# One decoder layer on one core: the SSM output moved behind the mask product, the merge's first loads split over two queues, the expert records loaded before the expert stage

## The reference, cut to what matters

```
h = rms_norm(x)
proj = h @ w_in                        # all branch inputs and 3 x 1024 gate logits
y_gla, y_hgrn = chunked gated linear attention (8 heads, per-channel decays)
y_ssm = rms_norm((ssd_scan(xs, dt, B, C) + d * xs) * silu(z))   # Mamba-2, 16 heads
merged = sum over 3 branches of sigmoid(gates[b]) * (y_b @ w_br_b)
x = x + merged @ w_out
h = rms_norm(x)
x = x + top-2-of-32 experts (group top-1, then 2 of 8), SwiGLU, weighted
out = rms_norm(x)
```

## Time and profile before

| | us |
|---|---|
| median of 3 runs | 2226.93 (2224.96 to 2229.48) |
| the profiled execution | 2230.12, its span 2228.3 |
| PE busy in the span | 1998.3 (90%) |
| DVE / ACT / POOL busy | 1325.1 / 940.3 / 367.8 |
| mean granted clock of PE, 1.0 = 2.4 GHz | 0.954 |

### The profile page before, as it was taken

How to read it: one execution, slowest core, us unless ns; L and a number is a source line. 1 busy time by engine, 2 the same in 40 slices (tenths; PEclk the granted TensorE clock), 3 DMA queues, 4 the chain that set the end, 5 groups by cost and what they waited for, 6 DMA issues and landing times. The chain is left out here.

```text
span 2228.3 us, 25317 instructions
## 1 busy us (share of the span) xinstructions
PE 1998.3 (90%) x10102; PEld 1664.4 (75%) x10103; DVE 1325.1 (59%) x1426; ACT 940.3 (42%) x1012; POOL 367.8 (17%) x209
## 2 busy tenths in 40 slices
PE   4999999999989999989997999985599999999970
PEld 3778888888978777777775788775488888888860
DVE  4740000576115777767873665565599999999945
ACT  5120101112114433444442334242578888888842
POOL 3213323243410000000000100011122222222200
PEclk9999999999989999999998999997699999999995
DMA  4133222123235543654543754451799999999947
GB/s 154 59 144 102 98 91 95 59 93 132 76 101 144 144 136 115 158 140 144 148 133 126 259 210 185 150 220 48 255 370 381 387 387 387 390 385 385 388 181 264
DMA packets 218988, 435.85 MB, mean 196 GB/s; under 512 B 30770, under 2 KB 153666, under 8 KB 191234
## 3 DMA queue, kind: packets, MB, share of 16 engines
q1 hardware_dynamic: 185698, 354.63, 45.9%
q10 hardware_dynamic: 21152, 54.53, 6.7%
q0 software_dynamic: 12032, 25.22, 3.0%
HBM read 369.67 MB, written 81.43 MB: 202 GB/s over the span
## 5 line engine op out<-in xcount | busy, mean ns | idle before, releaser
L583 DVE TENSOR_SCALAR tap<-u,taps 128x1024 f32<-128x1024 f32 x16 | 20.1, 1298 | 294.0 <-ACT u L541 294.0
L613 PE MATMUL ps<-h_hi,w_hi 128*128 128x512 f32 x576 | 178.4, 391 | 4.8 <-PEq L58 4.8
L613 PE MATMUL ps<-h_lo,w_hi 128*128 128x512 f32 x576 | 178.4, 391 | 0.0
L613 PE MATMUL ps<-h_hi,w_lo 128*128 128x512 f32 x576 | 178.3, 391 | 0.0
L2296 DVE TENSOR_TENSOR gu_lo<-gate_raw,gu_hi 128x2048 fp32r<-128x2048 f32 x64 | 146.7, 2293 | 48.1 <-ACT gu_hi L2243 48.1
L1247 PE MATMUL psum<-h_hi,l_hi 128*128 128x512 f32 x384 | 160.5, 418 | 7.3 <-PEq L58 7.3
L1247 PE MATMUL psum<-h_lo,l_hi 128*128 128x512 f32 x384 | 161.0, 419 | 0.0
L1247 PE MATMUL psum<-h_hi,l_lo 128*128 128x512 f32 x384 | 160.6, 418 | 0.0
L2296 DVE TENSOR_TENSOR gu_lo<-up_raw,gu_hi 128x2048 fp32r<-128x2048 f32 x64 | 146.3, 2288 | 13.4 <-ACT gu_hi L2243 13.4
L2301 DVE TENSOR_TENSOR dn_lo<-dn_raw,dn_hi 128x2048 fp32r<-128x2048 f32 x62 | 142.0, 2292 | 16.0 <-ACT dn_hi L2253 13.0
L551 ACT ACTIVATE out<-ps 128x2048 f32<-128x2048 f32 x14 | 26.4, 1883 | 271.1 <-PE ps L613 202.1
(11 more groups left out here) (352 smaller groups left out, 5024.3 us busy)
## 6 DMA issues: line engine op xcount, KB each, us to landing
gate_raw<-moe SPq DMA_DIRECT2D x66, 1024.0 KB, 8.8
up_raw<-moe SPq DMA_DIRECT2D x64, 1024.0 KB, 8.4
dn_raw<-moe SPq DMA_DIRECT2D x62, 1024.0 KB, 7.8
w_raw<-w_in SPq DMA_DIRECT2D x26, 1024.0 KB, 6.7
dn_raw<-w_br SPq DMA_DIRECT2D x16, 1024.0 KB, 7.5
l_raw<-w_gates ACTq DMA_DIRECT2D x24, 512.0 KB, 4.9
s_gates<-l_out ACTq DMA_DIRECT2D x48, 256.0 KB, 4.0
gate<-s_gates SPq DMA_DIRECT2D x16, 768.0 KB, 5.4
```

The source lines that it names most:

```text
L583: ins = nc.vector.tensor_scalar(tap[:, a, :], u[b][:, a, 0:T], taps[b][:, a, 0:1], None, ALU.mult)
L613: ins = nc.tensor.matmul(ps[b][:, a * T + half * 512:a * T + half * 512 + 512], w[:, k, a * P:(a + 1) * P], h[:, k, half * 512:half * 512 ...
```

## The change

It has four parts.

1. `mixers`: DVE's `ssm_out(c - 1)` moves from ahead of the `k_in` product to behind the mask product `wmat * cbm`; DVE waits for its own `yb_ready` before it overwrites `yt`. On PE one of the two slots of fill that stood behind the `k_in` transposes moves ahead of them.
2. Start of `merge_and_route`: step 0's weights are loaded and split in two halves; the eight first-half y pieces get eight buffers of their own (pieces 4 to 7 in `xh`) and eight semaphores, the even ones issued by ACT and the odd ones by SP, with no wait; POOL issues the second half's pieces only. The table is filled from `h2T` instead of `xh[0]`.
3. Routing on ACT: the first `exps` moves behind the last sigmoid, and a table set that holds both Ln and Exp is preloaded before it.
4. `recs` becomes a buffer that outlives the block: SP loads it at the end of `merge_and_route`, after the last scatter, as two transfers (experts 0 and 1, then the other 30). In the expert block ACT no longer waits for it, POOL waits for the first part only, and DVE zeroes `xe` instead of POOL.

```diff
@@ mixers, DVE
                 dec(i0 + 8)
-                if c:
-                    ssm_out(c - 1)
                 dve.wait_ge(e_ready, NE * c + NE)
...
                 tt(w4, w4, cbm[:]...).then_inc(w_ready, 1)
+                if c:
+                    ssm_out(c - 1)
                 dec(i0 + 9)
                 dec(i0 + 10)
...
                 dve.wait_ge(inter_ready, c + 1)
+                if c:
+                    dve.wait_ge(yb_ready, c)
@@ mixers, PE
                 level(c, 6)
-                fill(SLOT)
+                fill(2 * SLOT)
...            # six transposes of k_in
-                fill(2 * SLOT)
+                fill(SLOT)
@@ merge_and_route, SP
-            weights(0)
+            sp.dma_start(first(w0_raw), first(io["w_br"][0])).then_inc(w0_loaded, 16)
+            y_piece(sp, 1)
+            y_piece(sp, 3)
+            sp.dma_start(second(w0_raw), second(io["w_br"][0])).then_inc(w_loaded[0], 16)
+            y_piece(sp, 5)
+            y_piece(sp, 7)
             weights(1)
...
             sp.wait_ge(work_stored, 16)
+            sp.wait_ge(scattered, 16 * 2 * NCH)
+            places = dr["table"].rearrange("(e s) w -> s e w", s=T)[0:SLAB]
+            sp.dma_start(recs[:, 0:2, :], places[:, 0:2, :]).then_inc(recs_first, 16)
+            sp.dma_start(recs[:, 2:N_EXPERTS, :], places[:, 2:N_EXPERTS, :]).then_inc(recs_in, 16)
@@ merge_and_route, ACT
+            for p in range(0, PIECES, 2):
+                y_piece(act, p)
             nc.scalar.preload_act_table(ACT.Sigmoid)
...
                 upper_w(step_of(n) + 2)
-                if n == 2 * DM - 2:
-                    exps(0)
+            nc.scalar.preload_act_table_set(EXP_LN_SET)
+            exps(0)
@@ experts_first_slabs
-            sp.dma_start(recs[:], dr["table"]...).then_inc(recs_in, 16)      # SP
-            for b in range(2):                                               # POOL
-                nc.gpsimd.memset(xe[b][:], 0.0).then_inc(zeroed, 1)
-            pool.wait_ge(recs_in, 16)
+            pool.wait_ge(recs_first, 16)
-            act.wait_ge(recs_in, 16)                                         # ACT, ahead of gate_up(0, 0)
+            for b in range(2):                                               # DVE
+                nc.vector.memset(xe[b][:], 0.0).then_inc(zeroed, 1)
```

More of the change, by code:

```diff
@@ L1542, in merge_and_route, with y_piece @@
         block = ctx.enter_context(nc.Block())
+        def y_piece(eng, p):
+            half, q = divmod(p, PIECES)
+            if half:
+                eng.wait_ge(y_ready, p - 7 if p < PIECES + 4 else p - 3)
+            eng.dma_start(y_part(p), dr["y"][q * PK * P:(q + 1) * PK * P, half * HT:(half + 1) * HT]
+                          .rearrange("(k p) t -> p k t", p=P)).then_inc(y_second[p % 4] if half else y_first[p], 16)
+        W0 = 8 * P
+        first = lambda t: t[:, 0:W0]
+        second = lambda t: t[:, W0:2048]
+        w0_raw = w_raw[0][:].rearrange("p k n -> p (k n)")
         @block.sync
@@ L1632, in _ @@
         def _(pool):
[L1633 to L1644, removed]
+            nc.gpsimd.memset(h2T[:].rearrange("p k t -> p (k t)").bitcast(U32), EMPTY).then_inc(empty_ready, 1)
             nc.gpsimd.iota(it32[:], pattern=[[1, N_EXPERTS]], base=0, channel_multiplier=0, allow_small_or_imprecise_dtypes=True).then_inc(const_ready, 1)
@@ L1701, in upper_w, with upper_w0 @@
                 nc.scalar.copy(out, w_raw[s % 2][:].rearrange("p k n -> p (k n)")).then_inc(w_hi_ready, 1)
+            def upper_w0(part, loaded, ready):
+                act.wait_ge(loaded, 16)
+                nc.scalar.copy(part(w_hi[0][:]), part(w0_raw)).then_inc(ready, 1)
             def upper_y(p):
-                act.wait_ge(y_loaded[p % 4], 16 * (p // 4 + 1))
+                if p < PIECES:
+                    act.wait_ge(y_first[p], 16)
+                else:
+                    act.wait_ge(y_second[p % 4], 16 * ((p - PIECES) // 4 + 1))
                 if p >= PIECES:
@@ L1741, in exps @@
                 nc.scalar.activation(e2[:, 0:n], e2[:, 0:n], ACT.Exp).then_inc(pick_exp, 1)
-            upper_w(0)
-            for p in range(PIECES):
+            upper_w0(first, w0_loaded, w0_hi_ready)
+            for p in range(4):
+                upper_y(p)
+            upper_w0(second, w_loaded[0], w_hi_ready)
+            for p in range(4, PIECES):
                 upper_y(p)
@@ L1891, in places, with rest_w0 @@
                     nc.vector.tensor_copy(rec[:, pick, cs, 2].bitcast(F32), w[:, 0:n]).then_inc(rec_ready, 1)
-            rest_w(0)
-            for p in range(PIECES):
+            def rest_w0(part, hi_ready, ready):
+                dve.wait_ge(hi_ready, 1)
+                tt(part(w_lo[0][:]), part(w0_raw), part(w_hi[0][:]).bitcast(F32), ALU.subtract).then_inc(ready, 1)
+            rest_w0(first, w0_hi_ready, w0_ready)
+            for p in range(4):
+                rest_y(p)
+            rest_w0(second, w_hi_ready, w_ready)
+            for p in range(4, PIECES):
                 rest_y(p)
@@ L2324, in body @@
                                         hT_hi[:].rearrange("p k t -> p (k t)").bitcast(F32), ALU.subtract).then_inc(hT_split, 1)
+            for b in range(2):
+                nc.vector.memset(xe[b][:], 0.0).then_inc(zeroed, 1)
             for p in range(GU):
```

51 lines of the change are left out of this document (32 added, 19 removed).

## The result

| | before | after |
|---|---|---|
| median, us | 2226.86 (4 runs, 2224.96 to 2229.48) | 2202.31 (4 runs, 2196.90 to 2209.94) |
| the profiled execution, its span | 2230.12, 2228.3 | 2209.94, 2208.2 |
| mean granted clock of PE | 0.954 | 0.958 |

The ratio is 0.9887 with a 95% interval of 0.9866 to 0.9907, so 20.7 to 29.8 us less, 25.2 by the ratio itself. The profiled execution after the change is the slowest of its four; the trace therefore shows a gain of 20.2 us where the medians differ by 24.6. What sets it apart from the fastest is mostly PE's clock. Call (1 - granted clock) x span the clock deficit of an execution: it is 92.7, 92.5, 85.7 and 79.0 us in the four executions of 2209.94, 2204.91, 2199.72 and 2196.90 us. The ratios further down leave out two of merge_only's twelve executions (2650 and 6410 us), which were disturbed, and no others.

The account below looks back on a forecast made before the run. PE, busy for 90% of the span, was taken as the bound, with time won only in its waits or low clock. Terms 15.0 + 6.2 - 2 + 6 + 2.6 + 4 = 31.8 us off 2226.93 gave 2195 (range 2184 to 2211).

Parts of the forecast that it names:

- (a): In mixers, a fill slot ahead of the k_in transposes shrinks PE's gap: 1.87 us a chunk, 15.0 us gained.
- the gap only moves: Rival for mixers: the score copy ends too late, so (a) and (c) give nothing: 2216 us, chance 0.06.
- (b): In mixers, moving DVE's SSM output behind the mask product neither gains nor costs: 0 us.
- (c): In mixers, shorter gaps before the k_in transposes remove low PE clock in four chunks: 6.2 us gained.
- (d): In mixers, the later store of yb delays the wmat load and so cbm: 2 us lost.
- slower: Rival for mixers: yb's store delays wmat by 5.0 us in all seven chunks, 35 us: 2239 us, chance 0.04.
- (e): At the merge's start, fewer bytes ahead bring the first matmul and step 1 sooner: 6 us gained.
- the merge stays bound by bytes: Rival for the merge: step 1's weights share DMA engines with 2.1 MB coming sooner, (e) gives 0: 2201 us, chance 0.12.
- (f): In routing's last chunk, two table loads before the norm vanish: 2.6 us gained.
- (g): At the experts' start, ACT no longer waits for records, so PE starts sooner: 4 us gained.

Follow-up runs that it names:

- merge_only: Kernel before with only the edits to the first loads of the merge (part 2): 2228.72 against 2228.73 us, ratio 0.9996.
- fill_only: Kernel before with only one slot of PE fill moved ahead of the k_in transposes: 2208.67 against 2228.73 us, ratio 0.9914.
- ssm_only: Kernel before with only DVE's SSM output moved behind the mask product: 2230.44 against 2228.73 us, ratio 1.0008.
- experiment 3: Kernel before with DVE's wd moved behind cbm, 2229.72 against 2228.62 us; also tables of clock deficits and of PE gaps followed by low clock.
- mix_only: Kernel before with both mixers edits (fill slot and SSM output) and nothing else: 2207.81 against 2228.73 us, ratio 0.9909.
- experiment 2: No run of its own: DVE's wmat waits compared across eleven traces, yb's store at its old or new place; means 11.5 and 11.4 us.
- after_pool_late: Changed kernel with POOL's second-half y pieces and the table's filling held back at the merge: 2200.24 against 2230.68 us (kernel before), ratio 0.9863.
- after_one_queue: Changed kernel with SP issuing all eight first-half y pieces, none on ACT: 2204.19 against 2228.62 us (kernel before), ratio 0.9894.
- recs_only: Kernel before with only the edits to the records (part 4): 2226.24 against 2230.68 us, ratio 0.9984.
- after_rows_first: Changed kernel with expert 0's gathered rows split ahead of its two up pieces: 2197.73 against 2228.62 us (kernel before), ratio 0.9872.
- exps_only: Kernel before with only the first exps moved and the table set preloaded (part 3): 2227.89 against 2230.68 us, ratio 0.9985.
- before_wd_late: Kernel before with only wd and its exponentials moved behind cbm: 2229.72 against 2228.62 us, ratio 1.0007.

## Why the prediction came out as it did

The forecast was 2195 (range 2184 to 2211), 31.8 us less; measured were 2202.31 and 25.2 us less by the ratio. Direction, range and the largest terms were right. The gains of the merge, of the table loads and, by the profile, of the records were taken too large, and one loss can't be seen. In the order of its terms:

- **(a) The slot of fill, 15.0 us.** Right to the row: the gaps went from 21.7 to 6.6 us over the eight chunks, the gap of the chunk worked out from 2.48 to 0.60 (0.61 forecast), the way from the transposes to the output products to 2.59 us (2.59 forecast). In time, fill_only's gain holds 14 us that are not clock, near the 15.0. So the rival that the gap only moves is out.
- **(b) The SSM output, 0.** Right: ssm_only shows no gain.
- **(c) The clock, 6.2 us.** The mechanism holds (the tables of experiment 3): the stretches of low clock in `mixers` begin at gaps from about 2 us up, PE's gaps ahead of `k_in` no longer reach that, and the clock deficit fell by 5.9 us in fill_only and 8.5 in mix_only. But the profiled execution of the changed kernel has two long stretches behind `cbm` gaps of 2.81 and 4.25 us, so the sum there falls only from 8.5 to 6.8 us; in mix_only, with `cbm` gaps of at most 1.1 us, it falls to 0. "No gap below 2.4 us is followed by it" was too narrow a reading of one trace: over all of them a gap of 1.99 and one of 2.05 us are.
- **(d) The store of `yb`, 2 us lost.** Not shown. In the profile `cbm`'s waits did grow by 2.7 us, which looks like a hit, but experiment 2 shows the same spread with the store at its old place. The cost can't be told from 0, nor from 2: ssm_only allows 1.3 us faster to 5.1 slower. The term should have been a spread, not a loss. The rival "slower", with its 35 us, is out.
- **(a) to (d) together**: 19.2 us forecast; 20.3 (16 to 25) by the timing of mix_only.
- **(e) The merge, 6 us.** The largest error, in two steps. First, the start: the first matmul at 8.5 us (8 forecast) was right, but step 1 comes 3.1 us sooner instead of 6, as its weights land late. after_pool_late shows the cause that the rival "the merge stays bound by bytes" named: with POOL's 2.1 MB and the table behind them, step 1 comes 5.5 us sooner. Second, the clock: PE stands idle for 3.27 us ahead of step 1 (0.31 before), and the stretch of low clock behind that gap gives 1.6 of the 3.1 us back. The gates that SP issues behind step 1 come 48.5 us behind the block's start before and 47.1 after (1260.46, 1245.70), and PE has no idle time between. This corrects what the expectation of merge_only says: the weights of step 2 are late (cast at 1231.72), but PE never waits for them. The sum had not asked what PE's gap at step 1 would do to the clock. The last `x2` is 2.7 us sooner, 1.8 in merge_only, whose timing shows 0.9 us (-2.7 to 4.5): between the rival's 0 and the forecast, nearer to the rival. The rule of the Trainium skill that was weighed there ("DMA: Bandwidth & Descriptors", section "Issuing engines are not separate DMA queues") holds in after_one_queue, where the second issuing engine is gone and nothing comes later by more than 0.2 us: 8.65 and 29.85 us from one queue, 8.54 and 29.66 from two.
- **(f) The table loads, 2.6 us.** The mechanism was right and its size was 1.6 us, since I had not asked what is late next: the store of `x2` ends the wait.
- **(g) The records, 4 us.** In the profile 2.9 us (20.5 less 17.6), 2.55 of them behind the experts' start (19.29 to the first matmul before, 16.74 after); 3.6 (1.1 to 6.0) by the timing of recs_only. ACT's first cast starts 1.29 us behind the block's start (1547.83), with no wait for records, 7.28 before; that is 6.0 us sooner where 5.2 was forecast, since the barrier came no later. From the last store to the start it is 6.93 us, 7.27 before, not 0.8 more. What was late next is in-order work: `xeT_lo` behind the second `gu_lo` of `up_raw` (1559.80), behind a transfer; after_rows_first turned the order round and the way from the transposes to the first expert matmul fell by 1.5 us. And the gather took longer: from its issue to the transposes 8.8 us (1548.65, 1557.43) instead of 5.4 (1572.66, 1578.09). It now runs beside the loads of `up_raw`; that these slow it was not tried.

The parts apart (mix_only, merge_only, exps_only, recs_only) add up to 20.3 + 0.9 + 3.3 + 3.6 = 28.1 us, the whole to 25.2, within the spread of each. Most of the total is the gain of `mixers`, which was forecast term by term; the smaller parts are each near the limit of what the timing can tell.

## What to carry to other kernels

When a wait is shortened, ask at once what ends it next: here a store's landing, a split queued behind a transfer, and a gap with low clock behind it took back a part of each of three terms. Independent work moved ahead of a late operand is worth its full length only as long as the gap it fills is open, and more than that where the gap was long enough to bring the clock down with it; work off the path, like the SSM output, showed no worth at either place. One trace is one draw: the same block differed by up to 10 us between traces of kernels that share its code, so a term that depends on a landing or on the clock wants several traces before it gets a sign.

## What the runs showed of the hardware

- In `mixers` a stretch at a granted clock of 0.50 costs 1.70 or 3.41 us, in all 39 stretches of fourteen traces. None began at one of the 113 PE gaps between 0.8 and 1.8 us, and 27 of the 36 gaps over 2.6 us had one behind them, so the same gap brings the clock down in one execution and not in another.
- Because of it a wait can be removed with no gain (before_wd_late: 3.5 us less of the rest and 4.8 us more of clock deficit over 12 and 17 executions, ratio 1.0007), and a start moved forward can lose half its worth (step 1 of the merge: 3.1 us sooner, 1.6 given back behind a gap of 3.27 us).
- A large part of the spread between executions of one kernel is clock: the four of the changed kernel span 13.0 us of time and 13.7 us of clock deficit, and over 23 of the kernel before the two correlate at 0.83.
- SP's issues at the start of the changed kernel's merge took 6.40 us for two gates, 5.93 for the table and 1.82 for a weight, against 0.37 (gate) and 0.49 (weight) further on. What slows them was not tried; the kernel before, with fewer transfers issued ahead, took 1.46 us for its two gates and 0.35 for the table.
- DVE's wait for the 1 MB load of `wmat`, summed over seven chunks, was 9.9, 10.4, 13.3 and 14.3 us in four traces with the same code up to there (after_one_queue, after_rows_first, the changed kernel, after_pool_late).
